# First block's gate: operand parts, waits by bank, and the place of two side chains

## The reference, cut to what matters

```python
p_l = modulate(rmsnorm(h_lat, norm1[i]), sh1_l, sc1_l) @ w_in[i]     # "xn" @ w_in
z, xs, bm, cm, dt_f, dt_b = ssd_inputs(p_l, ...)
y, s_f, s_b = ssd_bidir(xs, bm, cm, dt_f, dt_b, a_f, a_b, h0_f, h0_b)  # the scan
y = y + xs * d_skip
y = group_rmsnorm(y * silu(z), norm_g, SSD_GROUPS)                    # the gate
u = dwconv_centred(proj_hy, short_w, short_b)                         # the short filters
# hyena_filters: h = sin(f0 * (zpos @ w1 + b1)); h = sin(f1 * (h @ w2 + b2)); h = h @ w3 ...
```

## Time and profile before

| what | value |
|---|---|
| median of three runs | 4749.26 us |
| the profiled execution | 4758.25 us |
| its span, first to last instruction | 4756.4 us |
| TensorE (PE) busy | 4534.2 us, 95% |
| VectorE (DVE) busy | 2632.0 us, 55% |
| ScalarE (ACT) busy | 1549.1 us, 33% |
| POOL busy | 1484.0 us, 31% |
| mean granted clock of TensorE | 0.964 |

### The profile page before, as it was taken

One profiled execution on the slowest core, in us unless ns is written; L12 is line 12 of the kernel. 1 busy time (PEld: TensorE's weight loads), 2 busy tenths in 40 slices (PEclk: granted clock), 3 DMA queues, 4 the chain that ended last, 5 costly groups with the idle time before them and its releaser, 6 DMA issues.

```text
span 4756.4 us, 55821 instructions
## 1 busy us (share of the span) xinstructions
PE 4534.2 (95%) x22471; PEld 3762.7 (79%) x22471; DVE 2632.0 (55%) x3690; ACT 1549.1 (33%) x2151; POOL 1484.0 (31%) x962
## 2 busy tenths in 40 slices
PE   7999899999989999999999988999999999999998
PEld 4757755779989999999888755788788778887887
DVE  5655667559869988888522356422322355444223
ACT  3324211233335543333322333322322242123222
POOL 1033023314887657788410100210211101122101
PEclk8999999999999999999999998999999999898999
DMA  4142321224876789999522221222222221002222
GB/s 170 45 137 95 117 84 47 89 90 154 261 241 216 260 335 390 374 372 396 186 94 93 80 71 36 69 96 93 85 93 93 89 94 61 23 6 81 96 93 76
DMA packets 228972, 663.48 MB, mean 139 GB/s; under 512 B 22170, under 2 KB 87978, under 8 KB 226539
## 3 DMA queue, kind: packets, MB, share of 16 engines
q1 hardware_dynamic: 112832, 398.15, 24.2%
q0 software_dynamic: 38752, 143.03, 8.2%
q10 hardware_dynamic: 77128, 118.73, 6.9%
HBM read 591.66 MB, written 68.16 MB: 139 GB/s over the span
## 4 chain that ended last, share of the span: by engine, by line
PE 75%; DVE 11%; POOL 3%; ACT 2%; issue 2%; DMA 1%; ACTq 0%; DVEq 0%; SPq 0%; POOLq 0%
PE ps L257 19%; PE ps L258 18%; PE ps L259 18%; PE ps L1464 2%; DVE r L226 2%; DVE A L1893 2%; PE ps L581 1%; PE ps L1543 1%; DVE A L2192 1%; DMA A<-acts 1%; PE ps L3262 1%; POOL r L226 1%; PE ps L3269 1%; DVE A L2193 1%; ACT r L220 1%
## 5 line engine op out<-in xcount | busy, mean ns | idle before, releaser
L257 PE MATMUL ps<-r,r 128*128 128x512 f32 (+2 forms) x5160 | 1933.8, 375 | 32.2 <-POOL r L226 11.6
L258 PE MATMUL ps<-r,r 128*128 128x512 f32 (+2 forms) x5160 | 1917.2, 372 | 0.0
L259 PE MATMUL ps<-r,r 128*128 128x512 f32 (+2 forms) x5160 | 1916.4, 371 | 0.0
L226 DVE TENSOR_TENSOR r<-A,r 128x1024 fp32r<-128x1024 f32 x589 | 790.2, 1342 | 1434.4 <-ACT r L220 1424.7
L220 ACT ACTIVATE r<-A 128x1024 fp32r<-128x1024 f32 x665 | 704.1, 1059 | 1724.8 <-PE ps L259 1554.3
L257 PEld LDWEIGHTS ps<-r,r 128*128 128x128 f32 x5160 | 974.7, 189 | 180.0 <-issue 26.8
L258 PEld LDWEIGHTS ps<-r,r 128*128 128x128 f32 x5160 | 974.6, 189 | 137.7 <-issue 3.4
L259 PEld LDWEIGHTS ps<-r,r 128*128 128x128 f32 x5160 | 973.5, 189 | 137.1
L276 POOL TENSOR_TENSOR r<-A,r 128x512 fp32r<-128x512 f32 (+2 forms) x305 | 406.6, 1339 | 1441.0 <-ACT r L273 1284.9
L273 ACT ACTIVATE r<-A 128x512 fp32r<-128x512 f32 (+1 forms) x264 | 150.7, 579 | 458.8 <-DVE A L2266 265.4
L226 POOL TENSOR_TENSOR r<-A,r 128x1024 fp32r<-128x1024 f32 x76 | 204.2, 2689 | 140.3 <-ACT r L220 139.4
(11 more groups left out here) (501 smaller groups left out, 4707.6 us busy)
## 6 DMA issues: line engine op xcount, KB each, us to landing
A<-in_pu SPq DMA_DIRECT2D x128, 512.0 KB
A<-in_pv SPq DMA_DIRECT2D x128, 512.0 KB
A<-in_f1i SPq DMA_DIRECT2D x88, 512.0 KB
A<-in_f2i SPq DMA_DIRECT2D x88, 512.0 KB
A<-in_w_mod SPq DMA_DIRECT2D x48, 512.0 KB
A<-in_w_in SPq DMA_DIRECT2D x48, 512.0 KB
acts<-A ACTq DMA_DIRECT2D x128, 192.0 KB
gates<-A ACTq DMA_DIRECT2D x8, 3072.0 KB, 11.2
```

Source lines behind the costliest of these rows:

```text
L226: e.tensor_tensor(self.vr(at + 1024, 1024), self.v(self.st0 + 1024 * (u % RS), 1024), self.vr(at, 1024).bitcast(F32), ALU.subtract).then_i ...
L257: t.matmul(o, hi, xh, start=first and k == k0, stop=False)
L258: t.matmul(o, hi, xl, start=False, stop=False)
L259: m = t.matmul(o, lo, xh, start=False, stop=final and k == K - 1)
```

## The change

The tile 7 of `xn` goes to the buffer of the modulation's rows (`L.ROW`), tile 6 behind the scan's storage, so both can be fetched within `prod`. The hi and lo parts are made within `prod` as the storage that they overwrite comes free. The waits for the end of `prod` are gone: each z group waits for what still holds its bank. The five loads go behind z 0 on ScalarE. The gate's last factor and its scaling go into iterations 0, 2 and 3 of `short`, ScalarE's loads and store there into iteration 5, and the second hidden layer behind group 9 (TensorE), ahead of filter 10 (VectorE) and behind product 10 (ScalarE), its copies to iteration 12. No arithmetic is added or removed.

```diff
-        L.XR = [L.BTOK + 512 * k for k in range(6)] + [self.al(512) for k in (6, 7)]
+        self.top = L.AL + 32
+        L.XR = [L.BTOK + 512 * k for k in range(6)] + [self.al(512), L.ROW]
...
     def prod_s(self, s):
         for o in range(2, 5):
             self.weights_s(s, 32)
+        s.wait_ge(*S.at("modtr", 11))
+        for k in (6, 7):
+            s.dma_start(self.v(L.XR[k], 512), self.xnd[:, 512 * k:512 * k + 512]).then_inc(...)
...
     def prod_a(self, a):
-        self.end("a", "prod")
+        a.wait_ge(*S.at("cb", 3))
+        for k in range(8):
+            a.wait_ge(*S.at("xn back", k))
+            if k == 6:
+                a.wait_ge(*S.at("queries", 31))
+            self.part_hi(a, self.v(L.XR[k], 512), L.XN2 + 512 * k, 512, "xn hi", k)
...
     def prod_v(self, v):
+        v.wait_ge(*S.at("queries", 31))
+        for k in (0, 1):
+            self.gate_lo(v, "v", k)
+        v.wait_ge(*S.at("products", 15))
+        for k in (2, 3):
+            self.gate_lo(v, "v", k)
         self.y_v(v, 7)
         self.modcol_v(v, 2, 32, "norm2")
-        self.end("v", "prod")
+        for k in (5, 6):
+            self.gate_lo(v, "v", k)
...
     def prod_g(self, g):
-        self.end("g", "prod")
+        g.wait_ge(*S.at("products", 15))
+        for k in (4, 7):
+            self.gate_lo(g, "g", k)
...
+    def gate_lo(self, e, who, k):
+        S, L = self.S, self.L1
+        e.wait_ge(*S.at("xn hi", k))
+        self.part_lo(e, who, self.v(L.XR[k], 512), L.XN2 + 512 * k, L.XN2 + 4096 + 512 * k, 512, "xn lo", k)
...
     def gate_t(self, t):
-        self.after(t, "t", "prod")
         for o in range(8):
-            if o >= 4:
+            if o < 2:
+                t.wait_ge(*S.at("y", 6 + o))
+            elif o == 2:
+                t.wait_ge(*S.at("cbm", 3))
+            elif o == 3:
+                t.wait_ge(*S.at("decay", 30))
+                t.wait_ge(*S.at("decay min", 30))
+            else:
                 t.wait_ge(*S.at("z", o - 4))
...
-            if o in (3, 6):
-                self.mlp_t(t, o // 3 - 1)
+            if o == 3:
+                self.mlp_t(t, 0)
...
     def gate_a(self, a):
-        self.after(a, "a", "prod")
-        self.mlp_load_a(a)
...
+            if o == 0:
+                self.mlp_load_a(a)
...
     def short_t(self, t):
+            if o == 9:
+                self.mlp_t(t, 1)
...
     def turn_t(self, t, o):
+        if o == 1:
+            t.wait_ge(*S.at("ms", ("ssd", 3)))
...
     def short_v(self, v):
-        self.after(v, "v", "gate")
...
+            if o == 10:
+                self.mlp_v(v, 1)
+            if o == 12:
                 v.wait_ge(*S.at("layer", 1))
...
+            if o == 0:
+                self.gate_ms_v(v, 3)
+            if o == 2:
+                self.rstd_v2(v, self.gate_r(3), ("ssd", 3))
+            if o == 3:
+                self.gate_scale_v(v, 3)
+                self.end("v", "gate")
...
     def short_a(self, a):
-        self.after(a, "a", "gate")
-        self.load_filter(a, 0)
-        a.dma_start(self.hxd, self.v(L.OS, 4096)).then_inc(*S.dma("osk", "scan kept"))
...
+            if o == 0:
+                self.rstd_a(a, self.gate_r(3), ("ssd", 3))
+            if o == 5:
+                self.after(a, "a", "gate")
+                self.load_filter(a, 0)
+                a.dma_start(self.hxd, self.v(L.OS, 4096)).then_inc(*S.dma("osk", "scan kept"))
+            if o == 10:
+                self.mlp_a(a, 1)
```

More of the change, by code:

```diff
@@ L1012, in prod_s @@
             self.weights_s(s, 32)
+        s.wait_ge(*S.at("modtr", 11))
+        for k in (6, 7):
+            s.dma_start(self.v(L.XR[k], 512), self.xnd[:, 512 * k:512 * k + 512]).then_inc(*S.dma(f"xnr{k}", "xn back", k))
     def prod_t(self, t):
@@ L1044, in prod_t @@
         self.products_t(t, 15)
-        self.end("t", "prod")
     def products_t(self, t, h):
@@ L1143, in prod_g @@
                     g.tensor_tensor(dm, dm, self.v(L.WKB + 1024 * (q % 2), 512), ALU.mult).then_inc(*S.on("g", "weights", n))
-        self.end("g", "prod")
+        g.wait_ge(*S.at("products", 15))
+        for k in (4, 7):
+            self.gate_lo(g, "g", k)
     def gate_s(self, s):
         S, L = self.S, self.L1
-        self.after(s, "s", "prod")
-        for k in (6, 7):
-            s.dma_start(self.v(L.XR[k], 512), self.xnd[:, 512 * k:512 * k + 512]).then_inc(*S.dma(f"xnr{k}", "xn back", k))
         for o in range(8):
             self.weights_s(s, 8)
+    def gate_lo(self, e, who, k):
+        S, L = self.S, self.L1
+        e.wait_ge(*S.at("xn hi", k))
+        self.part_lo(e, who, self.v(L.XR[k], 512), L.XN2 + 512 * k, L.XN2 + 4096 + 512 * k, 512, "xn lo", k)
     def gate_norm_t(self, t, q):
@@ L1169, in gate_t @@
                 self.gate_norm_t(t, o // 2 - 1)
-            if o in (3, 6):
-                self.mlp_t(t, o // 3 - 1)
+            if o == 3:
+                self.mlp_t(t, 0)
     def gate_a(self, a):
         S, L, PS = self.S, self.L1, self.PS
-        self.after(a, "a", "prod")
-        self.mlp_load_a(a)
-        for k in range(8):
-            a.wait_ge(*S.at("xn back", k))
-            self.part_hi(a, self.v(L.XR[k], 512), L.XN2 + 512 * k, 512, "xn hi", k)
         for o in range(9):
@@ L1191, in gate_a @@
                 self.rms_a(a, [self.v(L.CHX + 512 * i, 512) for i in (o - 1, o)], 512, L.WK + 1024, ("ssd", q), [("gated", o - 1), ("gated", o)])
-            elif o:
+            elif 0 < o < 8:
                 self.rstd_a(a, self.v(L.WK + 2048 + 512 * ((q - 1) % 2), 512), ("ssd", q - 1))
@@ L1195, in gate_a @@
                 self.mlp_a(a, 0)
-            if o == 8:
-                self.mlp_a(a, 1)
         self.end("a", "gate")
@@ L1201, in gate_v @@
         S, L = self.S, self.L1
[L1202 to L1220, removed]
+        for o in range(8):
+            self.weights_v(v, 8)
+            y = self.v(L.CHX + 512 * o, 512)
+            v.wait_ge(*S.at("z", o))
+            v.tensor_tensor(y, y, self.v(L.WK + 512 * (o % 2), 512), ALU.mult).then_inc(*S.on("v", "gated", o))
+            if o in (2, 4, 6):
+                q = o // 2 - 1
+                self.gate_ms_v(v, q)
+                self.rstd_v2(v, self.gate_r(q), ("ssd", q))
+                self.gate_scale_v(v, q)
@@ L1221, in gate_v, with gate_r @@
             if o == 3:
                 self.mlp_v(v, 0)
-            if o == 7:
-                self.mlp_v(v, 1)
-        self.end("v", "gate")
-    def gate_g(self, g):
[L1228 to L1232, removed]
+    def gate_r(self, q):
+        return self.v(self.L1.WK + 2048 + 512 * (q % 2), 512)
@@ L1233, in gate_g, with gate_ms_v, gate_scale_v @@
+    def gate_ms_v(self, v, q):
+        self.rstd_v(v, 2, 512, 1.0 / 256, 1e-6, self.gate_r(q), ("ssd", q), 4 + q % 2)
+    def gate_scale_v(self, v, q):
+        S, L = self.S, self.L1
+        v.wait_ge(*S.at("rstd", ("ssd", q)))
+        for i in (2 * q, 2 * q + 1):
+            y = self.v(L.CHX + 512 * i, 512)
+            v.scalar_tensor_tensor(out=y, in0=y, scalar=self.prm("ssd_norm", i), in1=self.gate_r(q), op0=ALU.mult, op1=ALU.mult).then_inc(*S.on("v"))
+    def gate_g(self, g):
         for o in range(8):
```

## The result

The changed kernel takes 4737.19 us (median of 7 runs, 4729.46 to 4747.85), the kernel before 4750.05 (median of 7). The ratio is 0.9967 with a 95% interval of 0.9955 to 0.9980, so 9 to 21 us less. Forecast were 4733 us and a range of 4725 to 4743. The profiled execution has a span of 4743.3 us, 13.1 less than before's.

The account below looks back on a forecast made before the run. TensorE, busy 95% of the span, was taken as the bound, so only its idle or slow-clock time can be won. Terms of 5.9 and 10.4 us sum to 16.3: from 4749.26 to 4733 us, range 4725 to 4743.

Parts of the forecast that it names:

- The first term: Gate's start: 5.9 us won, from 5.1 of idle time and 2.1 of slow clock gone, 1.3 of new small waits.
- rival A: First z group: stalls longer, parts 2 to 7 contended and clock down, 3.7 us instead of 5.9; chance 0.15.
- Waits by bank: TensorE's z groups: each waits for what last holds its bank, all earlier than their groups; cost 0.
- The five DMA issues: ScalarE behind z 0: 2.6 us of issues, just covered by its 2.61 us of idle time; cost 0.
- The layer: Second layer moved behind short group 9: VectorE's 4.7 us hidden by idle time there; cost 0, without that cover 4.7 us.
- The last factor: Before the first turn, factor moved into the short groups: 8.93 us wait goes, 1.5 us of slow clock with it.
- rival B: Turns 2 and 3: reciprocal and scaling make them late, second hole moves, its term falls to 4 us; chance 0.1.
- The sum: Gate's start and end together: 5.9 + 10.4 = 16.3 us less, taken as 16.
- rival C: Later in the kernel: a wait that doesn't shift gives back half of the gain, 4741 us; chance 0.07.
- Rival D: Behind 560 us: the shift changes where the clock falls, up to some 2.1 us per wait, kernel slower; chance 0.05.

Follow-up runs that it names:

- start_only: The changed kernel with second layer and last factor back in the gate, so only the gate's start is changed; ratio to the kernel before 0.9978.
- lo_on_v: The changed kernel with all six late subtractions on VectorE, none on POOL; 76.3 us from the scan's last product to the third turn, one run.
- layer_in_gate: The changed kernel with the second layer put back behind z group 6; 79.3 us from the scan's last product to the third turn, one run.
- end_only: The kernel before with only the gate's end changed (second layer, last factor, ScalarE's loads and store moved into the short filters); ratio to it 0.9968.
- factor_in_gate: The changed kernel with last factor, scaling and ScalarE's loads and store put back ahead of the short filters; ratio to the kernel before 0.9982.

## Why the prediction was right

- **The first term, 5.9 us.** At the end of z group 0 the changed kernel has gained 6.3 us: the next group starts 13.1 us behind the last product's start before (438.26 less 425.2) and 6.8 after (429.78 less 423.0). `start_only` keeps 6.1 of it at the third turn and 5.9 over the stretch; that the last figure is the forecast's is partly luck. The first z product starts right behind the last scan product. Group 0 has two small waits rather than three. Without them (`lo_on_v`) the third turn is 0.9 us earlier, so they cost 0.9 us, not 1.3. The size was off because I gave each subtraction 1.6 us: VectorE's pair took 2.40 us and not 3.2, POOL's 3.51 about as I had it. The slow clock of group 0 was 2.04 us by its own numbers (7.63 less 5.59), not 2.1. The clock stayed at 1.00 in the group, as I took it to; rival A did not come.
- **Waits by bank, 0.** No wait before z groups 1 to 3 in the waits of after.
- **The five DMA issues, cost 0.** Right, but not by the cover that I named. The issues run at 430.12 to 432.69, beside ScalarE's weights, table load and Silu, and ScalarE still idles 2.61 us ahead of 435.62, exactly as in the earlier trace rows. They took nothing of that idle time.
- **The layer, cost 0.** Right for the change as a whole: no new wait of TensorE stands in its waits up to 560 us. Alone its place is worth a wait of 0.6 us and 1.0 us by the third turn, by `layer_in_gate`.
- **The last factor, 8.9 and 1.5 us.** The first turn waits for nothing and the clock stays up. `end_only` gives 10.8 to the third turn without the layer's pass, against 10.4. The reciprocal runs between turn 1's copy and the next weights, and the fourth turn still starts in cadence:

```profile
499.55 3.34 DVE L308 RECIPROCAL A<-A 128x512 f32<-128x512 f32 x1
502.81 1.16 DVE L226 TENSOR_TENSOR r<-A,r 128x1024 fp32r<-128x1024 f32 x1
...
505.91 0.68 DVE L1361 COPY A<-ps 128x512 f32<-128x512 f32 x1
```

  Filter 3 is done at 505.9 and the turn that needs it starts at 506.25, 6.05 behind the third: 0.3 us of slack, as worked out. So rival B did not come.
- **The sum, 16.3 us.** 16.2, 17.2 and 17.2 in three profiles of the changed kernel. By the third turn all three have gained 17.0 without the layer's pass (18.1 less 1.1), so the forecast was 0.7 us low; the 16.2 comes from the longer slow clock behind the last turn in that profile, which nobody edited.
- **The time.** 4733 forecast, 4737.19 measured, with 4732.72 and 4735.76 in the repeats. The difference is the size of the spread between sets of runs. Of rival C nothing was seen: the part behind is not longer on the whole (4120.2, 4111.2 and 4111.0 against 4114.9), and the means of the three sets of runs are 14.0, 24.9 and 16.8 us below before's, none of them as little as the 8 us that C leaves. Rival D did not come, but what it builds on shows between two profiles of the changed kernel. Ahead of the scan's first product, and from it to the last, the first profile has

```profile
0.00:295.80 295.80, 247.45 (x1149) 170.81 (x1150) 182.12 (x253) 104.76 (x236) 48.84 (x42) 0.92 0.33 115
295.80:423.00 127.20, 121.91 (x843) 94.19 (x842) 62.05 (x161) 41.62 (x70) 56.60 (x45) 0.96 0.29 96
```

  and the second

```profile
0.00:302.10 302.10, 252.31 (x1149) 173.09 (x1150) 182.07 (x253) 104.76 (x236) 48.89 (x42) 0.91 0.33 112
302.10:431.80 129.70, 123.49 (x843) 95.71 (x841) 62.00 (x161) 41.66 (x70) 56.55 (x45) 0.95 0.28 94
```

  These are the same instructions, and they take 8.8 us longer. TensorE is busy 6.4 us longer with as many matmuls, at a lower granted clock, and stands idle 2.4 us longer.
  This fits the rule of the Trainium skill cited in the prediction ("TensorE: Matmul & The Clock Gate", "What's actually happening"): the same program meets the slow stretches at other places from one execution to the next.

## What to carry to other kernels

Where one engine is busy 95% of the time, look for its holes, and price each as its idle time plus the slow clock behind it. Two holes in series, with work between them that this engine bounds, added here (6.1 and 11.9 us alone, 18.1 together). A short side chain (a norm's last factor, a load, a hidden layer) should stand behind work that the bounding engine can already do; here its place needed only that the slack of one cadence, 2.19 + 1.5 us, covers its longest instruction, 3.35. Judge an edit of a few microseconds by the distance between two marks around it in the profile: here it repeats within 1 us, while the part behind them alone moves by 21 us, and a profile with the hole put back (`factor_in_gate`, 4739.6 us) had a shorter span than one of the change (4743.3).

## What was not expected of the hardware

- When VectorE and POOL both subtract from 423.35 us on, they do not share evenly. Of VectorE's six subtractions in the kernel after, five take about 0.68 us and one 1.79:

```profile
L276 DVE TENSOR_TENSOR r<-A,r x6: 678/680/1792, 419.4 to 427.5; 128x512 fp32r<-128x512 f32 x6
```

  Even the tiny instruction behind `y` takes 0.60 us there and 0.16 in `lo_on_v`; it ends about when POOL's second subtraction does, at 426.90. `y` itself, which reads PSUM, takes its usual 0.73 beside it. On VectorE alone each subtraction takes 0.69 at most. POOL's two take 1.75 to 1.81 us each, where its shortest in the earlier trace rows is 1.28. The Trainium skill ("GPSIMD Engine Reference", "Specifications") names such a contention for VectorE instructions with two SBUF inputs; the rows agree, and put the price at 1.1 us for one of two 512-column subtractions.
- ScalarE's queue issues DMAs while its earlier instructions still run: the issue at 430.12 us stands behind the Silu in the program and is over two microseconds ahead of it (432.41) in time. Issues cost ScalarE's time where the instruction behind them is ready to go: in `factor_in_gate` the first is at 496.69 us, and the weights behind them start at 499.12.
